# A tenth slot for expert rows and two instead of three places for weight units, in a two-layer decoder trunk with retrieved experts

## What is computed

```python
q = (ht @ w_query).reshape(T, PEER_HEADS, D_KEY)
s1, s2 = q halves against the two tables of 128 sub-keys
v1, i1 = lax.top_k(s1, PEER_TOPK)
v2, i2 = lax.top_k(s2, PEER_TOPK)
sc, ci = lax.top_k(all sums v1 + v2, PEER_TOPK)
e_idx = i1[ci // 16] * N_KEYS + i2[ci % 16]
gate = jax.nn.softmax(sc)
a = einsum('chkd,cd->chk', expert_u[ec], xc)
w = gelu(a) * gc
x += einsum('chk,chkd->cd', w, expert_v[ec])
```

## Time and profile before

| | |
|---|---|
| median of 3 runs | 2944.4 us (2943.28 to 2945.59) |
| profiled execution | 2945.85 us |
| its span | 2944.1 us |
| PE (TensorE matmul) busy | 2348.5 us, 80% |
| DVE (VectorE) busy | 2011.5 us, 68% |
| ACT (ScalarE) busy | 1252.6 us, 43% |
| POOL (GpSimd) busy | 1224.8 us, 42% |
| DMA | 1192.25 MB, mean 405 GB/s |
| chain that ended last | DMA 46%, PE 30%, DVE 10%, ACT 7% |
| granted TensorE clock | 0.835 of full, mean |

### The profile page before, as it was taken

How to read it: one execution, slowest core, us unless ns; L and a number is a source line. 1 busy time by engine, 2 the same in 40 slices (tenths; PEclk the granted TensorE clock), 3 DMA queues, 4 the chain that set the end, 5 groups by cost and what they waited for, 6 DMA issues and landing times.

```text
span 2944.1 us, 37736 instructions
## 1 busy us (share of the span) xinstructions
PE 2348.5 (80%) x12436; PEld 938.3 (32%) x12436; DVE 2011.5 (68%) x4762; ACT 1252.6 (43%) x3713; POOL 1224.8 (42%) x1063
## 2 busy tenths in 40 slices
PE   9889888998958988787976897888896676666665
PEld 7634444344512332242421333323341111111110
DVE  2677667886478757877458767787547777777554
ACT  2333633953334337633334435753334333333333
POOL 0333343444334434444334433444434444545443
PEclk9999887998968997897977999888897766676665
DMA  9699999999999999999999999999999999999996
GB/s 359 270 358 397 386 405 414 420 420 419 413 418 417 411 417 418 417 408 420 417 415 405 414 414 421 409 387 420 420 420 421 419 422 421 421 412 421 421 422 290
DMA packets 202348, 1192.25 MB, mean 405 GB/s; under 512 B 25384, under 2 KB 38184, under 8 KB 68520
## 3 DMA queue, kind: packets, MB, share of 16 engines
q0 software_dynamic: 147456, 1073.81, 88.4%
q1 hardware_dynamic: 54696, 116.03, 10.5%
HBM read 1187.67 MB, written 2.10 MB: 404 GB/s over the span
## 4 chain that ended last, share of the span: by engine, by line
DMA 46%; PE 30%; DVE 10%; ACT 7%; issue 5%; POOL 1%; SPq 0%; POOLq 0%; DVEq 0%; ACTq 0%
DMA arena<-in_uv,eidx 43%; PE acc L1863 12%; PE bank L1544 8%; DVE arena L1528 5%; PE bank L1789 4%; PE bank L1626 3%; DMA unit<-in_w_in 2%; ACT L1076 2%; POOL arena L835 1%; ACT wts L1079 1%; ACT diag L1087 1%; ACT L968 1%; PE heads L1544 1%; ACT gelu L1076 1%; DMA unit<-in_w_query 1%
## 5 line engine op out<-in xcount | busy, mean ns | idle before, releaser
L835 POOL DMA_INDIRECT arena<-in_uv,eidx x1024 | 1189.3, 1161 | 1527.4 <-PE acc L1863 1263.7
L1863 PE MATMUL acc<-arena,diag 64*64 64x512 f32 x7984 | 1370.7, 772 | 537.0 <-ACT diag L1087 505.0
L1528 DVE CUSTOM_DVE_ANT_0 arena<-arena,h 128x1024 f32<-128x1024 f32 x1024 | 1254.9, 1226 | 745.9 <-DMA arena<-in_uv,eidx 738.8
L1076 ACT ACTIVATE gelu<-dots 128x1 f32<-128x1 f32 x1024 | 206.2, 201 | 1393.8 <-DVE dots L1528 1392.3
L1863 PEld LDWEIGHTS acc<-arena,diag 64*64 64x64 f32 x7984 | 249.2, 156 | 1353.4 <-ACT diag L1087 1179.3
L1087 ACT ACTIVATE diag<-identc,wts 128x64 f32<-128x64 f32 x998 | 347.0, 348 | 33.4
L1079 ACT ACTIVATE wts<-gelu,gate 128x1 f32<-128x1 f32 x1024 | 301.5, 294 | 34.1
L1789 PE MATMUL bank<-h,unit 128*128 128x256 f32 (+1 forms) x1024 | 230.9, 372 | 7.8 <-DMA unit<-in_w_query 7.8
L1789 PEld LDWEIGHTS bank<-h,unit 128*128 128x128 f32 x1024 | 172.3, 197 | 116.0 <-issue 91.6
L1544 PE MATMUL bank<-unit,h 128*128 128x512 f32 (+1 forms) x336 | 138.2, 541 | 0.0
L1626 PE MATMUL bank<-h,unit 128*128 128x256 f32 (+2 forms) x480 | 122.2, 398 | 0.0
(11 more groups left out here) (211 smaller groups left out, 1783.7 us busy)
## 6 DMA issues: line engine op xcount, KB each, us to landing
unit<-in_w_in SPq DMA_DIRECT2D x36, 1024.0 KB, 21.6
unit<-in_w_query SPq DMA_DIRECT2D x35, 1024.0 KB, 12.4
arena<-in_uv,eidx POOLq DMA_INDIRECT x1024, 17.3
unit<-in_w_out SPq DMA_DIRECT2D x16, 1024.0 KB, 9.8
arena<-in_w_in SPq DMA_DIRECT2D x8, 1024.0 KB, 11.5
arena<-in_w_query SPq DMA_DIRECT2D x5, 1024.0 KB, 19.9
arena<-in_w_out SPq DMA_DIRECT2D x4, 1024.0 KB, 14.9
x<-in_x SPq DMA_DIRECT2D x4, 512.0 KB, 10.7
```

Of the source, the lines that this page charges most:

```text
L835: nc.gpsimd.indirect_dma_start(arena[:, n % NBUF, :], None, uv, bass.IndirectOffsetOnAxis(ap=eidx[:, seq % 2, j:j + 1], axis=0)).then_inc( ...
L1076: nc.scalar.activation(gelu[:, group], dots[:, group], ACT.Gelu_apprx_tanh).then_inc(s_ge, GROUP)
L1528: V.tensor_tensor_reduce(out=uu, in0=uu, in1=h_nat[seq % 3], scale=1.0, scalar=0.0, op0=ALU.mult, op1=ALU.add, accum_out=dots[:, n % BODY: ...
L1863: ins = nc.tensor.matmul(acc[rows][cols * HALF:(cols + 1) * HALF, :], diag[own, n % NBUF, :], arena[own, n % NBUF, D + f * 512:D + (f + 1) ...
```

## The change

The ring of expert rows gets ten places, and with it the small rings of dot products, gelus, weights and diagonals (`BODY`). The ring of weight units keeps two. So a gather waits for the sum ten slots before it, and a unit's load for the use of the unit two before it. Of the 23 first units, the two that lay in the third unit place (CB, and by the count of twelve homes also the last QY unit) lie in the new arena slot 9, so that the first gather into slot 9 waits for that last QY unit's products. The place of the layer's small tensors in SyncE's list was written as `UNITBUF - 1` and stays behind the third unit.

```diff
-NBUF = 9
-UNITBUF = 3
+NBUF = 10
+UNITBUF = 2
 RING = 4
...
-BODY = 9
+BODY = 10
 ACT_LAG, DVE_LAG, POOL_LAG = 3, 3, 8
...
     first_home = [("slot", 0), ("slot", 1), ("slot", 2), ("slot", 4), ("slot", 5), ("slot", 6), ("slot", 7), ("slot", 8),
-                  ("ring", 0), ("ring", 1), ("ring", 2), ("slot", 3)]
+                  ("ring", 0), ("ring", 1), ("slot", 9), ("slot", 3)]
...
-                    if k == UNITBUF - 1 and opens_layer(p):
+                    if k == 2 and opens_layer(p):
                         load_layer(p)
```

## The result

The changed kernel takes 2969.8 us (median of 7 runs, 2962.1 to 2983.4) against 2945.1 (7 runs, 2943.3 to 2946.3): ratio 1.0089, 95% interval 1.008 to 1.0098. That is slower by 24.6 us, on the side forecast, 9.8 us above the forecast of 2960 and inside the range. The runs scatter more than before: 21 us from lowest to highest, against 3.

What follows compares the result with a forecast made beforehand. DMA transfer at 420 GB/s was taken to bind most of the kernel, TensorE at 165 to 330 us. Terms -8 -1 +5.5 +7 +0.5 +8 +6 made +18 on 2944.4, 2962, rounded to 2960 us; range 2939 to 2984.

Steps and rivals of the forecast that it cites:

- Pass 1's inputs: 165 to 330 us, TensorE the bound: CI and CB in 1 KB pieces land late; +5.5 us, bounds +2 and +9.
- Queries: Pass 1's w_out and queries, 380 to 480 us: units used in 5.5 us land late; +7 us, bounds 0 and +17.
- Pass 2: 632 to 800 us: units wait 0 to 1.2 us each, six units; +0.5 us, bounds 0 and +4.
- Pass 3: Inputs, 937 to 1105 us: CC and CB late, constants moved later, gathers pause; +8 us, bounds 0 and +20.
- Pass 4: Inputs, 1640 to 1796 us: the same as pass 3 without the constants; +6 us, bounds 0 and +14.
- The waits: TensorE's waits: in_w_in from 12.6 to 40 to 80 us, in_w_query about 25, first CC product of passes 3 and 4 8 to 15.
- The constants: Pass 3: the layer's constants follow CC, moving from 815 to about 951 us; GpSimd's mask waits, gathers pause 4 to 10 us more.
- The tenth slot: 2.5 us of cover at each place where the queue runs dry while GpSimd waits for a sum; -8 us, bounds -10 and 0.
- The cap at the roots: At the 23 inverse roots GpSimd's lag of 8 steps keeps gathers from going further ahead; worth 0.
- The start: The tenth gather, issued at 114.22 us before, goes out 10.6 us later behind the last query unit; 0, bounds 0 and +4.
- rival A: Weights land in time or gathers in flight cover late units, so the kernel is faster, 2936 to 2939 us; chance 0.16.
- D: The waits bite in full and the ring cannot refill: +50, 2994 us, the case from 2975 up; chance 0.15.

Runs made afterwards that it cites:

- e2: The changed kernel with the layer's small tensors of pass 3 loaded behind its second unit instead of its third; 2978.5 us, ratio 1.0098.
- e5: The changed kernel itself, run again on another chip against the kernel before; 2978.5 us, ratio 1.0100.
- e1: The kernel before with its nine slots, but only two places of the unit ring used after pass 0; 2981.5 us, ratio 1.0111.
- e7: The kernel before with three unit places but eight expert slots instead of nine; 2949.9 us, ratio 1.0015.
- e9: The kernel before, unchanged but for GpSimd's lag for dense steps, 9 instead of 8; ratio 0.9996.
- e3: The changed kernel with each weight unit laid out by the host as 128 rows of 8 KB; 2947.9 us, ratio 0.9994.

## Why the prediction was right, point by point

*The sum.* Predicted +18 on the profiled execution, the span grew 23.8. That it came so near is in part luck, since two errors offset each other. The costs were taken at 27 us and came to 36.7. The gains were taken at 9 and came to 12.9, but 10 of these (6.4 in 1796 to 1988 and 3.6 in 1260 to 1640 us) are there with nine slots too: the slot was credited with what something else gave back.

*The costs* lie inside their bounds but for pass 1's inputs, 0.4 us over theirs. Pass 1's inputs: taken +5.5, bounds +2 and +9, the window lost 9.4 (5.9 in e2, 14.1 in e5). The wait for a unit of 1 KB pieces was forecast from the row of 18.7 us and came, 2.62 us for CI, which landed in 17.7; but a V unit landed late too (18.5 us for a forecast 13.8) and TensorE waited 4.63 us for it. CB had landed 1 us before V was issued, so V did not queue behind it; why it took 18.5 is not shown. In e5 the wait for CI alone was 11.7 us, in e1 and e2 3.6 and 3.7. Queries: taken +7, bound 17, measured 5.2+4.3 = 9.5. The working had 5 us of waits for w_out by the landing of w_query; w_out lands sooner (9.8 us) and no wait for it is left after the change. Pass 2: 0.5, measured about zero. Pass 3: taken +8, measured 10.0. Pass 4: taken +6, measured 7.8.

*The waits.* CC in pass 3 was forecast to wait 12.9 us; it waited 12.20. CB was to land at 1017; it began at 1029.45 in a stage that came 12.2 us later, so at 1017.2, by the first of the two ways that were named (CI in time, CB late). But "26 to 28 us late" was counted from 990, and the kernel before did not begin CB there either:

```profile
997.47 3.61 PE L1544 MATMUL bank<-h,unit 128*128 128x256 f32 x8 [5.28 <-DMA unit<-in_w_in]
```

Against this row the change made CB 19.8 us late, 2 of them through the lower clock behind the wait for CC, a cost that the working put at nothing. In pass 4 the wait for CC was 12.15. in_w_in was to cost 40 to 80 us of waits, it costs 52.7 at line 1544 and 9.9 at 1626; in_w_query was to be 25 and is 18.6.

*The constants.* The mechanism was right to the number (mask 9.0 us behind its root, forecast 5 to 10), and the gathers did pause that much more. The pause is not its price: in e2's trace, without it, the queue moves 3 to 6 us more in this stage, because the gathers behind the first would have waited for sums anyway, and the time shows no difference.

*The tenth slot.* Taken as -8. e1 against the change says 3 to 6, with overlapping intervals; e7 says 4.3 for the ninth, clear of noise. The dip of 1935 to 1965 was to be smaller and is gone, but not for the reason given: e1 has nine slots and lost it too. So -8 was too much, and probably right in sign.

*The cap at the roots* was read rightly as a limit of 8 steps, since the root of 986.20 still stands between the gathers; but e9 shows that lifting it brings nothing in the kernel before.

*The start.* The tenth gather waited 14.7 us for the last query unit (it went out at 125.21 instead of 114.22) and 105 to 165 us moved 419 GB/s, against 413 before. Cost 0, as taken, in this execution; in e2, the same code up to there, it was 391.

*The measurement of the Trainium skill*, "DMA: Bandwidth & Descriptors", Bandwidth, 1 MB in 6.15 us, would have given rival A. Here it takes an unfilled queue to come near it (6.0 us for a load issued at 182.8 us in the kernel before, where 175 to 200 us moved 291 GB/s); beside full gathers even 8 KB pieces take 9.0.

*Rival A* is refuted, *D* was near in pass 1's inputs only, since starved moments did serve weights sooner: CB in pass 4, behind the two waits, landed in 12.4 us. In the median in_w_in lands after 16.4 us now, against 21.6, but part of that is that with two places a unit seldom queues behind another: CC alone in pass 3 took 26.1, CI alone before 26.7.

## What to carry to other kernels

Take a prefetch ring's depth from landing time over time of use, at the stage with the shortest use and the smallest pieces, and with the landing measured beside the real traffic; the stage with one row tile decided half of this loss. Before giving up a place, shorten the landing: making each load one contiguous 8 KB run a partition was worth more than any exchange between the rings. Depth in the stream that already keeps DMA full buys only cover against pauses, a few microseconds here. And a wait is to be priced by what the queue misses behind it, not by its length.

## What the runs showed that was not expected

A 1 MB load beside a saturated gather queue lands in 26.7, 17.0, 12.1 and 9.0 us with pieces of 1, 2, 4 and 8 KB, while the total rate stays within 2% of 420 GB/s. An estimate from these four says how the two queues share: spread over 16 DMA engines, such a load is 64, 32, 16 or 8 pieces for each, and (26.7-17.0)/32, (17.0-12.1)/16 and (12.1-9.0)/8 make 0.30, 0.31 and 0.39 us for each further piece, whatever its size. An 8 KB piece of a gather takes one engine 8.19/(420/16) = 0.31 us. So a weight piece costs about as long as one gather piece, as if the engines took the two in equal numbers. The kernel before has a load that bears this out: the forget columns of w_in (line 687) are 32 KB in 1024 pieces of 32 bytes. In pass 2 it was issued 0.4 us behind a unit of w_query and landed so:

```profile
DMA to landing us min/median/max: 30.8/30.8/30.8
```

Less the 12 us of the unit ahead that is 19 us for 64 pieces on each engine, 0.3 us each, with hardly any bytes in them.

The kernels with late weights scatter more between runs of one program: 21 us in the change and in e1, 15 in e5, 10 in e2, against 3 to 7 for the kernel before and 4 in e3 (2945.8 to 2949.7). That the late weights are the reason is not shown; e7, without them, scattered by 10. And the dip at 1840 to 1990 us is absent in the four kernels whose inputs of pass 4 were starved before it (the change, e1, e2, e5), with nine slots or ten, and there in the others; no run here says why.
